# Experts' gate and up pieces of 1 MB by one two-row transfer in place of two one-row transfers

## The reference

```
def swiglu(t, w_gate, w_up, w_down):
    return (jax.nn.silu(t @ w_gate) * (t @ w_up)) @ w_down
...
    logits = (t @ router).astype(jnp.float32)
    top_v, top_e = lax.top_k(logits, TOP_K)
    top_w = jax.nn.softmax(top_v, axis=-1)
...
    xb = t[row_tok].reshape(n_blocks, MOE_BLOCK, D)
    def expert_block(args):
        xe, e = args
        return swiglu(xe, w_gate[e], w_up[e], w_down[e])
    yb = lax.map(expert_block, (xb, block_e)).reshape(rows, D)
    out = jnp.zeros_like(t).at[row_tok].add((yb * row_w[:, None]).astype(t.dtype))
```

## Time and profile before

| | |
|---|---|
| median of 3 runs | 1149.87 us (1149.31 to 1150.11) |
| the profiled execution | 1150.17 us |
| its span, first to last instruction | 1148.4 us |
| mean granted TensorE clock | 0.990 |
| transfers of 512 KB for up and for gate, chunks 0 and 1 | 128 and 128 |
| TensorE busy, share of the span | 95% |

### The profile page before, as it was taken

One profiled execution on the slowest core, in us unless ns is written; L12 is line 12 of the kernel. 1 busy time (PEld: TensorE's weight loads), 2 busy tenths in 40 slices (PEclk: granted clock), 3 DMA queues, 4 the chain that ended last, 5 costly groups with the idle time before them and its releaser, 6 DMA issues.

```text
span 1148.4 us, 15814 instructions
## 1 busy us (share of the span) xinstructions
PE 1091.8 (95%) x5739; PEld 828.3 (72%) x5739; DVE 700.6 (61%) x757; ACT 634.4 (55%) x757; POOL 308.4 (27%) x338
## 2 busy tenths in 40 slices
PE   7999999999999999999979999879999869999996
PEld 7888888888888877894338883228894228898895
DVE  4875564445659559982038980028981018988996
ACT  6877643444686866771037760026771027777775
POOL 9986100000298775572003002004002004000000
PEclk9999999999999999999999999999999999999998
DMA  9644975525244389999999999999999999999971
GB/s 303 193 147 139 400 286 191 194 75 181 75 142 155 121 305 412 395 376 346 405 413 408 404 413 408 406 413 409 402 413 408 377 414 408 390 415 410 384 314 57
DMA packets 116935, 359.07 MB, mean 313 GB/s; under 512 B 13518, under 2 KB 32136, under 8 KB 106624
## 3 DMA queue, kind: packets, MB, share of 16 engines
q1 hardware_dynamic: 111024, 344.17, 78.3%
q0 software_dynamic: 5664, 13.76, 3.5%
q10 hardware_dynamic: 176, 0.27, 0.1%
HBM read 352.17 MB, written 8.91 MB: 314 GB/s over the span
## 4 chain that ended last, share of the span: by engine, by line
PE 76%; SPq 7%; DMA 7%; DVE 4%; ACT 4%; issue 2%; DVEq 0%; ACTq 0%
PE bank L2766 9%; PE bank L2767 8%; PE bank L2768 8%; SPq L704 7%; DMA ring<-in_moe_w_up_dram 6%; PE bank L2826 5%; PE bank L2793 4%; PE bank L2795 4%; PE bank L2794 4%; PE bank L2244 4%; PE bank L2245 3%; PE bank L2246 3%; PE bank L2361 2%; DVE low L2120 2%; PE bank L2363 2%; PE bank L2264 2%
## 5 line engine op out<-in xcount | busy, mean ns | idle before, releaser
L2120 DVE TENSOR_TENSOR low<-ring,high 128x2048 fp32r<-128x2048 f32 x162 | 369.8, 2290 | 94.1 <-ACT high L1462 92.9
L1462 ACT ACTIVATE high<-ring 128x2048 fp32r<-128x2048 f32 x162 | 310.5, 1918 | 147.1 <-PE bank L2768 83.2
L2766 PE MATMUL bank<-high,uTh 128*128 128x512 f32 (+2 forms) x500 | 187.5, 375 | 16.1 <-DVE low L2120 15.7
L2767 PE MATMUL bank<-low,uTh 128*128 128x512 f32 (+2 forms) x500 | 185.1, 370 | 0.0
L2768 PE MATMUL bank<-high,uTl 128*128 128x512 f32 (+2 forms) x500 | 184.9, 370 | 0.0
L1040 ACT ACTIVATE high<-ring 128x2048 fp32r<-128x2048 f32 (+1 forms) x65 | 122.6, 1892 | 68.8 <-PE bank L2246 41.9
L827 POOL TENSOR_TENSOR low<-ring,high 128x512 fp32r<-128x512 f32 (+1 forms) x67 | 84.7, 1298 | 196.5 <-ACT high L1040 195.1
L2826 PE MATMUL bank<-ring,spare 128*64 128x512 f32 (+3 forms) x600 | 124.0, 546 | 10.6 <-DMA ring<-in_moe_w_gate_dram 6.4
L1567 DVE TENSOR_TENSOR low<-ring,high 128x2048 fp32r<-128x2048 f32 (+2 forms) x40 | 90.1, 2259 | 54.8 <-ACT high L1040 52.2
L2766 PEld LDWEIGHTS bank<-high,uTh 128*128 128x128 f32 x500 | 95.5, 191 | 35.1 <-DVE low L2120 21.3
L2157 DVE TENSOR_TENSOR moe_sg<-bank,moe_sg 128x512 f32<-128x512 f32 (+1 forms) x9 | 5.8, 647 | 169.1 <-ACT moe_sg L1524 169.1
(11 more groups left out here) (465 smaller groups left out, 2025.9 us busy)
## 6 DMA issues: line engine op xcount, KB each, us to landing
ring<-in_moe_w_down_dram SPq DMA_DIRECT2D x80, 1024.0 KB, 15.5
ring<-in_moe_w_up_dram SPq DMA_DIRECT2D x128, 512.0 KB
ring<-in_moe_w_gate_dram SPq DMA_DIRECT2D x128, 512.0 KB, 12.4
ring<-in_w_in_dram SPq DMA_DIRECT2D x36, 512.0 KB, 6.2
ring<-in_moe_w_up_dram SPq DMA_DIRECT2D x24, 768.0 KB
ring<-in_moe_w_gate_dram SPq DMA_DIRECT2D x24, 768.0 KB
ring<-in_ffn_w_up_dram SPq DMA_DIRECT2D x22, 512.0 KB, 6.5
ring<-in_ffn_w_gate_dram SPq DMA_DIRECT2D x22, 512.0 KB, 9.6
```

The lines of the kernel that those rows point to most:

```text
L1462: act.activation(high[:, p % SPLIT, :], moe_slot(p), ACT.Copy).then_inc(s["high_ready"], 1)
L2120: dve.tensor_tensor(low[:, p % SPLIT, :], moe_slot(p), high[:, p % SPLIT, :].bitcast(F32), ALU.subtract).then_inc(s["low_ready"], 1)
L2766: pe.matmul(o, xh[:, k, :], bh, start=(k == 0), stop=False)
L2767: pe.matmul(o, xh[:, k, :], bl, start=False, stop=False)
```

## The change

Each gate and up piece of chunks 0 and 1 is one transfer: for each of the 128 partitions two rows of 4 KB, in one access pattern of 128 x 2 x 1024 (`both(0, 1024)` is the whole slot seen as two rows). The number of semaphore increments of such a piece goes from 32 to 16, so `landed` has a new rule: 16 for everything of chunks 0 and 1 and for the first and last down piece of chunk 2, else 32. `split_high` takes the number of increments for expert 0's first pieces from `landed_of`.

```
 def landed(key):
 
-    return 16 if key[0] == "d" and key != ("d", 2, 1) else 32
+    return 16 if key[1] < 2 or key in (("d", 2, 0), ("d", 2, 2)) else 32
...
                         if c < 2:
-                            parts = [(dst[:, 1024 * k:1024 * (k + 1)], w[:, 2 * i + k, c0:c0 + 1024]) for k in range(2)]
+                            parts = [(both(0, 1024), w[:, 2 * i:2 * i + 2, c0:c0 + 1024])]
...
             def split_high(n, width=PIECE):
 
-                act.wait_ge(loaded[SLOT_OF[n]], 32 * FILL_OF[n])
+                act.wait_ge(loaded[SLOT_OF[n]], 32 * FILL_OF[n] if n < MOE0 else landed_of(0, n - MOE0))
```

## The result

The changed kernel takes 1143.77 us in the median of 5 runs (1143.33 to 1144.68), the kernel before, run beside it, 1149.87 (1149.26 to 1150.18). The ratio is 0.995, with a 95% interval of 0.9935 to 0.9964: 6.1 us, or 0.5%, faster. The forecast was 1149.3 with a range of 1147.0 to 1151.8, so the time lies outside it, by 3.2 us.

The account below looks back on a forecast made before the run. Transfers were taken to bound the kernel from 527 to 943 us, TensorE afterwards. Profiled 1150.17 us less 0.6 for closing packets is 1149.6; the median being 0.3 lower, the forecast was 1149.3 us, range 1147.0 to 1151.8.

Parts of the forecast that it names:

- What bounds the kernel: Experts' stage: transfers bound it from 527 to 943 us, TensorE from 943 on (busy 183.94 of 188 us).
- From 527 to 943 the DMA engines work without a pause: Experts' stage: the queue is never empty, so what a piece costs the engines is what job 6's first piece awaits.
- 376 to 415 GB/s from the sixteenth slice to the thirty-eighth: Experts' stage: the rate at which the 16 DMA engines were read to move data, from the profile page.
- Step 1: Gate and up transfers of chunks 0 and 1: 16 fewer closing packets a piece, 0.009 us of 2.564 saved.
- Step 2: From 527.3 us to job 6's first piece: 70 merged pieces count, at 0.009 us each 0.6 us.
- Step 3: SP's issues: a piece drops from 0.67 to some 0.41 us and a few register instructions go; worth nothing.
- Steps 4 and 5: Readers' waits (16 in place of 32) and queue room (17 packets an issue, not 9): both cost nothing.
- Rival B: Second transfers of gate and up pieces: each has a fixed cost; 1143.9 in full, 1146.9 at half; chance 0.15.
- 418 GB/s or more in the stretches of chunks 0 and 1: Full-queue gate and up transfers: the rate that would say a transfer has a fixed cost; forecast 410 to 411.
- Rival C: Gate and up pieces of chunks 0 and 1: second row 1.4 MB away costs up to 0.11 us, 1157.0; chance 0.10.
- Rival D: Jobs 2 to 6: coarser issue runs DMA engines dry, 0.86 us a dip, one more each gives 1153.6; chance 0.07.
- The chain's three landings stand 174 to 175.5 us apart as now: Sign for the profile after: spacing of the landings before the three full jobs that follow half jobs stays unchanged.

Follow-up runs that it names:

- 5: Kernel before, two transfers a piece, with SP's loop over one expert run six times (body 183) and later slot waits: 1145.27 us, ratio 0.996.
- 6: Changed kernel, one transfer a piece, with SP's loop over one expert run six times (body 143) and later slot waits: 1145.17 us, ratio 0.9958.
- 3: Kernel before, two transfers a piece, with SP's loop over the half and full jobs written out three times: 1146.29 us, ratio 0.9964.
- 4: Changed kernel, one transfer a piece, with SP's loop over the half and full jobs written out three times: 1145.92 us, ratio 0.9961.
- 1: Changed kernel with already reached waits, 80 instructions, put into SP's loop, body back at 366: 1149.67 us, ratio 1.0.
- 7: Changed kernel with 32 instructions of already reached waits added to SP's loop, body 318: 1150.33 us, ratio 1.0004.
- 8: Changed kernel with 240 instructions of already reached waits in ScalarE's half jobs, its body 133 to 373, SP untouched: 1151.68 us, ratio 1.0013.
- 11: Changed kernel with 16 instructions of already reached waits added to SP's loop, body 302: 1150.0 us, ratio 0.9999.
- experiment 2: Against the kernel before, only the up pieces of chunks 0 and 1 merged, gate pieces still two transfers, SP's body 334: 1149.94 us, ratio 1.0001.

## Why the prediction was wrong

- **What bounds the kernel: right.** From 527 to 943 transfers do, and the gain in the last landing reached the end: 6.4 us there, 6.4 in the span. Behind it nothing moved but one for one.
- **"From 527 to 943 the DMA engines work without a pause": wrong in a way that matters.** It was read from the mean of 16 engines. The piece waits for the slowest. Fifteen engines had up to 6 us of slack at the end, and I priced an average. The page was misread too: "376 to 415 GB/s from the sixteenth slice to the thirty-eighth" leaves out the nineteenth, which has 346 and holds the pause at 525 to 530; no term hangs on it.
- **Step 1, the packet price, 0.009 us a piece: not borne out as a gain.** The packets went as forecast, the rate rose by 1 GB/s as forecast, but the pair 5 and 6, where only the merge differs, gives 0.1 us instead of 0.6, and 3 and 4 give 0.4. Both pairs scatter by more than that, so 0.6 isn't excluded; 6.0 is. The Trainium skill (DMA: Bandwidth & Descriptors, Anatomy of one DMA), with its bubble of about one cycle for the semaphore write, is not told apart from the packet price by these runs: by it the term was nearly 0, and the pair gives 0.1.
- **Step 2, 70 pieces: right as a place, and empty.** The loss sat in the same pieces, but not in what they are made of.
- **Step 3 is the step that failed.** "A few register instructions go" was costed at nothing because SP is never what the DMA waits for. That is true of SP's time, and I stopped there. With the 32 issues that go, 48 register instructions go, 80 of the 366 of a loop's round, and that many decide whether the loop must be fetched again in each round, by the same DMA engines that carry the weights. Its real worth is the 6.1 us, but for the 0.1 to 0.4 of step 1. The row was on the page I read: q14 instruction, 35 packets. I took 0.1% of the engines' time for nothing.
- **Steps 4 and 5, waits and room in the queue: right.** No new wait, no new dip.
- **Rival B: right in its number (1143.9) by luck, wrong in its reason.** Its sign, 418 GB/s or more in the stretches of chunks 0 and 1, didn't come (410), and experiments 1, 7, 8 and 11 keep its transfers, experiment 2 half of them, and all lose its gain. Read by the time alone, it would have been taken for confirmed.
- **Rival C: didn't happen.** The second row, 1.4 MB away, costs nothing that the 410 GB/s would show.
- **Rival D read the right row for the wrong thing.** The dip at 900 to 910 isn't made by the two-row issue beside it. The issues are the same in the changed kernel, and the dip is gone; it comes where one engine is 6 us behind.
- **"The chain's three landings stand 174 to 175.5 us apart as now"** was the sign that failed first, and it shows the place at once.

The Trainium skill (Runtime: NRT & Kernel Launch, Instruction fetch mechanics) says that a taken branch whose target isn't in the window held forces a fetch by DMA before execution goes on; SP's stop of 5.2 us at the loop's edge at 655.91 agrees. It also calls the cost of going from one block of code to the next "mostly hidden", and says that kernels prefer full unrolling where they can, as a branch can force such a fetch. In these runs the first is true of the engine at most, and not of the transfers: written out, SP has no pause of 5 us at an edge, and yet the kernels are 2.5 and 2.1 us over the changed one (experiments 3 and 4). The second holds for the loop that was fetched in each round (3.6 us gained) and not for the one that wasn't (2.1 us lost).

## What to carry to other kernels

Where transfers bound the end, look at each engine's instruction packets in the table of DMA queues, and ask of every edit to a loop how long its body becomes on each engine: here 286 instructions on SP cost no fetch per round and 302 cost five, and with them 6 us. A bulk transfer is as late as its slowest DMA engine, so compare the last landing with the last but one before you trust a mean rate. And when a time comes out as a rival said, look for that rival's own sign: an edit that keeps its cause and puts back something else, like 16 idle instructions, settles it for little.

## What the hardware showed that I had not expected

- Fetches of code for SP and ScalarE go by one queue (q14) in packets of 8 KB. A packet takes 0.31 us in the median, and by the landings a fetch sets one DMA engine back by 0.5 us (experiment 3) to 0.75 us (kernel before) where the queues are full. In these kernels it is the same engine each time, or the lag would not add up to 6.1 us as it does in the table of landings. Why a fetch costs up to twice its packet's time and more isn't settled.
- The limit lies between 286 and 302 instructions of SP's body. It is a step: 302, 318, 334 and 366 all have five fetches in the second stretch and take 1149.67 to 1150.33 us. The bodies of 286, 302 and 318 start at the same place in SP's code; whether the limit moves with the place where a loop starts wasn't tried.
- For ScalarE a body of 133 leaves it at no fetch in the second stretch, and 373 gives five; its limit between them wasn't looked for. Queue q8, also named "instruction", carries 36 packets of 16 KB in both kernels, four of them between the first and the third landing of the chain, the last at 681. Whose they are and what they cost wasn't tried.
